# Summing a gate's 128 partial rows with adding transfers instead of a product with ones, and moving two column sums to a later stage

## The reference

```python
mod = jax.nn.silu(c) @ w_ada[l] + b_ada[l]
sh_m, sc_m, gt_m, sh_f, sc_f, gt_f = [m[:, None, :] for m in jnp.split(mod, 6, axis=-1)]

h = rms_norm(x, g_pre_mix[l]) * (1.0 + sc_m) + sh_m
proj = h @ w_in[l]
...                      # attention on one half, convolution on the other
mix = jnp.concatenate([y_attn, y_conv], axis=-1) @ w_out[l]
x = x + gt_m * rms_norm(mix, g_post_mix[l])

h = rms_norm(x, g_pre_ffn[l]) * (1.0 + sc_f) + sh_f
ff = peer_ffn(h, peer_wq[l], ...)   # query projection h @ peer_wq, then expert lookup
x = x + gt_f * rms_norm(ff, g_post_ffn[l])
```

## Time and profile before

| | |
|---|---|
| time, median of 3 runs (range) | 1759.13 us (1758.56 to 1760.4) |
| the profiled execution | 1760.12 us, span 1758.1 us |
| busy: PE, DVE, ACT, POOL | 99%, 87%, 45%, 34% |
| read from HBM over the span | 598.19 MB, 350 GB/s in the mean |

### The profile page before, as it was taken

How to read it: one execution, slowest core, us unless ns; L and a number is a source line. 1 busy time by engine, 2 the same in 40 slices (tenths; PEclk the granted TensorE clock), 3 DMA queues, 4 the chain that set the end, 5 groups by cost and what they waited for, 6 DMA issues and landing times.

```text
span 1758.1 us, 28277 instructions
## 1 busy us (share of the span) xinstructions
PE 1732.3 (99%) x9480; PEld 1517.9 (86%) x9480; DVE 1535.3 (87%) x2469; ACT 799.5 (45%) x1185; POOL 603.1 (34%) x413
## 2 busy tenths in 40 slices
PE   7999999999999999999999999999999999999998
PEld 5888888644999999999999999988888888888886
DVE  4668899967688898998999999989999999999997
ACT  3001222300545555556555555554455544555454
POOL 1000000011000388788688888613321211112110
PEclk9999999999999999999999999999999999999999
DMA  9999986699798777987899999999999999999994
GB/s 380 421 421 422 424 322 252 234 387 417 301 349 272 219 218 223 296 253 224 249 382 389 399 411 404 401 365 411 414 413 410 390 404 398 397 399 389 407 387 190
DMA packets 142648, 617.22 MB, mean 351 GB/s; under 512 B 45347, under 2 KB 45939, under 8 KB 87411
## 3 DMA queue, kind: packets, MB, share of 16 engines
q1 hardware_dynamic: 80530, 410.04, 60.0%
q0 software_dynamic: 55712, 202.52, 31.9%
q10 hardware_dynamic: 6336, 3.75, 0.7%
HBM read 598.19 MB, written 16.89 MB: 350 GB/s over the span
## 4 chain that ended last, share of the span: by engine, by line
PE 76%; DMA 9%; DVE 8%; POOL 4%; issue 2%; ACT 1%; DVEq 0%; ACTq 0%; POOLq 0%; SPq 0%
PE ps L1448 33%; PE ps L1110 14%; PE ps L1117 9%; DMA raw<-in_w_ada 7%; PE ps L1161 5%; PE ps L1331 5%; POOL weights L570 3%; PE ps L1172 2%; DVE raw L1547 2%; PE ps L1103 2%; PE ps L1277 2%; DMA early<-in_w_front 1%; DVE w_low L1489 1%; DVE big L1603 1%; POOL big L555 1%
## 5 line engine op out<-in xcount | busy, mean ns | idle before, releaser
L805 ACT ACTIVATE w_hi<-raw 128x1024 fp32r<-128x1024 f32 x444 | 468.8, 1059 | 458.6 <-PE ps L1448 187.4
L1489 DVE TENSOR_TENSOR w_low<-raw,w_hi 128x1024 fp32r<-128x1024 f32 x444 | 541.5, 1224 | 85.5 <-ACT w_hi L805 77.6
L570 POOL DMA_INDIRECT weights<-sel x192 | 366.0, 1906 | 69.2 <-issue 57.6
L1110 PE MATMUL ps<-a,w_hi 128*128 128x384 f32 x1920 | 383.9, 341 | 0.8 <-issue 0.8
L1110 PEld LDWEIGHTS ps<-a,w_hi 128*128 128x128 f32 x1920 | 326.9, 189 | 1.6 <-issue 1.0
L1448 PE MATMUL ps<-w_low,a 128*128 128x512 f32 x1024 | 273.8, 389 | 0.0
L1448 PE MATMUL ps<-w_hi,a 128*128 128x512 f32 x1056 | 268.1, 389 | 1.5 <-ACT big L918 1.5
L1117 PEld LDWEIGHTS ps<-a,w_low 128*128 128x128 f32 x1920 | 247.1, 191 | 2.6 <-DVE w_low L1489 2.3
L1117 PE MATMUL ps<-a,w_low 128*128 128x192 f32 x1920 | 248.2, 271 | 0.7 <-DVE w_low L1489 0.6
L1448 PEld LDWEIGHTS ps<-w_hi,a 128*128 128x128 f32 x1056 | 198.2, 188 | 42.6 <-ACT big L918 1.6
L1448 PEld LDWEIGHTS ps<-w_low,a 128*128 128x128 f32 x1024 | 192.3, 188 | 39.8
(11 more groups left out here) (240 smaller groups left out, 2008.2 us busy)
## 6 DMA issues: line engine op xcount, KB each, us to landing
raw<-in_peer_u SPq DMA_DIRECT2D x128, 1024.0 KB
raw<-in_peer_v SPq DMA_DIRECT2D x256, 512.0 KB
early<-in_w_front SPq DMA_DIRECT2D x56, 1024.0 KB, 11.4
raw<-in_w_ada POOLq DMA_DIRECT2D x48, 1024.0 KB, 9.6
raw<-in_w_ada SPq DMA_DIRECT2D x32, 1024.0 KB
raw<-in_peer_wq SPq DMA_DIRECT2D x16, 1024.0 KB
big<-in_w_gate_f POOLq DMA_DIRECT2D x16, 1024.0 KB, 6.0
weights<-third SPq DMA_DIRECT2D x16, 768.0 KB, 19.1
```

Of the source, the lines that this page charges most:

```text
L570: gp.indirect_dma_start(weight_elements, bass.IndirectOffsetOnAxis(ap=put_at[:, c:c + 1], axis=0), put_gate[:, c:c + 1], None, compute_op= ...
L805: act.activation(high_at(ph, j), raw[:, s % RING, :], ACT.Copy).then_inc(hi_ready, 1)
L1110: done = pe.matmul(ps[:, b % 2, 0:2 * TD].rearrange("p (m t) -> p m t", m=2), high_at(ph, j)[:, k * P:(k + 1) * P], a_pair[:, kc, :, 0:TD] ...
L1489: dve.tensor_tensor(w_low[:, s % RING, :], raw[:, s % RING, :], high_at(ph, j).bitcast(F32), ALU.subtract).then_inc(lo_ready, 1)
```

## The change

The products with ones go. Seven adding transfers, issued by POOL behind the loads 55 to 58, sum `acc_gate` to one row. ACT then moves this row to DRAM, reads it back as columns [128, 16], DVE multiplies it by the columns of `g_post_mix` (one instruction of [128, 16] instead of four of [128, 512]), ACT writes the product to DRAM and reads it back as a row on all partitions. `g_post_mix` is read as columns, so the copy `g_row` on all partitions goes.

The sums S30 and S31 (the last two blocks of `w_ada`, `DEFERRED = 2`) leave the ring: POOL loads them into `gate_in_ring` when the 78 others are used, and DVE sums them in the query projection, in the places of the first two gate steps; the gate steps move two places back, and two places later in the projection hold two steps each. S29 stands where S31 stood, behind the residual. `mod_columns` makes 15 of 16 columns at its old place and the last one in the projection. `peer_wq` block 1 now waits for S29, the last sum on its ring place.

```diff
+DEFERRED = 2
+N_RING = N_A - DEFERRED
+TWO_GATE_STEPS = (20, 28)
...
-                        sp.wait_ge(mod_used, N_A - SLOTS + block + 1)
+                        sp.wait_ge(mod_used, max(m for m in range(N_RING) if m % SLOTS == block) + 1)
...
-            for n in range(A_GATE, N_A):
+            for n in range(A_GATE, N_RING):
                 gp.wait_ge(mod_used, max(A_GATE, n - SLOTS + 1))
                 gp.dma_start(mod_slots[n % SLOTS], w_ada[n]).then_inc(mod_in[n % SLOTS], 16)
+                if 0 <= n - SLOTS + 1 - MOD_GATES < len(FOLDS_BEHIND):
+                    for fold in FOLDS_BEHIND[n - SLOTS + 1 - MOD_GATES]:
+                        if fold:
+                            gp.wait_ge(gate_sum_ready, 16 * fold)
+                        span = FOLDS[fold]
+                        gp.dma_start(acc_gate[0:span, :], acc_gate[span:2 * span, :], accum_op=ALU.add)\
+                            .then_inc(gate_sum_ready, 16)
...
+            gp.wait_ge(mod_used, N_RING)
+            for d in range(DEFERRED):
+                gp.dma_start(gate_in_ring[:, d % 2, :], w_ada[N_RING + d]).then_inc(gate_f_in[d % 2], 16)
             for g in range(KC):
                 if g < 2:
-                    gp.wait_ge(mod_used, N_A)
+                    gp.wait_ge(late_mod_used, LATE_MODS + DEFERRED + g - 1)
...
-            act.dma_start(g_row, rows[2, :].partition_broadcast(P)).then_inc(g_row_in, 16)
+            act.wait_ge(h_made_first, KC)
+            act.dma_start(mix_g, rows[2, :].rearrange("(p a) -> p a", p=P)).then_inc(g_row_in, 16)
...
             put_y(PAIRS - 1)
-            act.wait_ge(gate_made, 4)
             act.dma_start(gate_g[:, :], rows[3, :].rearrange("(p a) -> p a", p=P)).then_inc(g_row_in, 16)
+            act.wait_ge(gate_sum_ready, 16 * len(FOLDS))
+            act.dma_start(mix_gate_saved, acc_gate[0:1, :]).then_inc(gate_moved, 16)
+            act.wait_ge(gate_moved, 16)
+            act.dma_start(mix_gate, mix_gate_saved[0, :].rearrange("(p a) -> p a", p=P)).then_inc(gate_moved, 16)
+            act.wait_ge(gate_made, 1)
+            act.dma_start(mix_gate_saved[0, :].rearrange("(p a) -> p a", p=P), mix_gate).then_inc(gate_moved, 16)
+            act.wait_ge(gate_moved, 48)
+            act.dma_start(gate_row, mix_gate_saved[0, :].partition_broadcast(P)).then_inc(gate_moved, 16)
...
-            pe.wait_ge(mod_used, MOD_GATES)
             pe.wait_ge(ln_var, 1)
             pe.wait_ge(y_ready, PAIRS)
-            for g in range(4):
-                done = pe.matmul(ps[:, MIX_SECOND[g], :], ones[:, :], acc_gate[:, g * 512:(g + 1) * 512],
-                                 start=True, stop=True)
-            done.then_inc(gate_sum_ready, 1)
             mix_step(0, 7)
-            pe.wait_ge(gate_made, 4)
...
-            column_sums(10, 15)
-            dve.wait_ge(gate_sum_ready, 1)
-            dve.wait_ge(g_row_in, 16)
-            for g in range(4):
-                cols = slice(g * 512, (g + 1) * 512)
-                dve.tensor_tensor(gate_row[:, cols], ps[:, MIX_SECOND[g], :], g_row[:, cols], ALU.mult)\
-                    .then_inc(gate_made, 1)
-            column_sums(15, 22)
-            dve.wait_ge(gate_made, 4)
+            column_sums(10, 18)
+            dve.wait_ge(gate_moved, 32)
+            dve.wait_ge(g_row_in, 32)
+            dve.tensor_tensor(mix_gate, mix_gate, mix_g, ALU.mult).then_inc(gate_made, 1)
+            column_sums(18, 23)
+            dve.wait_ge(gate_moved, 64)
...
-            column_sums(22, 2 * KC - 1)
+            column_sums(23, 2 * KC - DEFERRED - 1)
...
-            column_sums(2 * KC - 1, 2 * KC)
+            column_sums(2 * KC - DEFERRED - 1, 2 * KC - DEFERRED)
             x2_variance(0)
             x2_diagonal(0)
-            mod_columns()
+            mod_columns(slice(0, K_RING), mod_used, N_RING)
...
-                gate_f_step(u - 4)
+                if u < FIRST_PLAIN + DEFERRED:
+                    late_column_sum(u - FIRST_PLAIN)
+                else:
+                    gate_f_step(u - FIRST_PLAIN - DEFERRED)
+                if u == FIRST_PLAIN + DEFERRED:
+                    mod_columns(slice(K_RING, KC), late_mod_used, LATE_MODS + DEFERRED)
```

More of the change, by code:

```diff
@@ L38 @@
 FOLDS = (64, 32, 16, 8, 4, 2, 1)
+FOLDS_BEHIND = ((0, 1), (2, 3), (4, 5), (6,))
 def at(i, step, first):
@@ L94 @@
 MOD_AT = {nth: n for n, nth in enumerate(MOD_ORDER)}
+DEFERRED = 2
+N_RING = N_A - DEFERRED
+K_RING = KC - DEFERRED // 2
+TWO_GATE_STEPS = (20, 28)
+LATE_MODS = CONV_CHUNKS
 MIX_FIRST, MIX_SECOND = (0, 1, 4, 5), (2, 3, 6, 7)
@@ L192, in build_block @@
         gate_row = region(25984, D)
-        g_row = region(28032, D)
         keysT = region(30080, 2, KEYS)
@@ L282, in build_block @@
         gate_cols = macc[:, 0, :]
+        mix_g, mix_gate = modc[:, 0, :], modc[:, 1, :]
         lam_sum, lam_exp, neg_lam = tiny[:, 0:2], tiny[:, 2:4], tiny[:, 4:5]
@@ L324, in build_block @@
             sem("ln_n"), sem("z_ready"))
-        gate_sum_ready, gate_made = sem("gate_sum_ready"), sem("gate_made")
+        gate_sum_ready, gate_made, gate_moved = sem("gate_sum_ready"), sem("gate_made"), sem("gate_moved")
         mix_first = sem("mix_first")
+        late_mod_used = glu_ready
         mix_sq, mix_gated, m_var, m_root = sem("mix_sq"), sem("mix_gated"), sem("m_var"), sem("m_root")
@@ L842, in _ @@
             x2_sqrt(0)
-            act.wait_ge(mod_used, N_A)
+            act.wait_ge(mod_used, N_RING)
             act.wait_ge(mod_f, 1)
@@ L859, in high_chunk @@
                 act.wait_ge(turned, k + 1)
+                if k == K_RING:
+                    act.wait_ge(late_mod_used, LATE_MODS + DEFERRED)
+                    act.wait_ge(mod_f, 2)
                 cols = slice(P if k < FIRST_PLAIN else 0, T)
@@ L1548, in column_sum, with late_column_sum @@
                                          macc[:, group, k:k + 1]).then_inc(mod_used, 1)
+            def late_column_sum(d):
+                nth = MOD_ORDER[N_RING + d]
+                group, k = (nth // A_FFN) * 2 + nth % 2, (nth % A_FFN) // 2
+                dve.wait_ge(gate_f_in[d % 2], 16 * (d // 2 + 1))
+                dve.tensor_tensor_reduce(gate_in_ring[:, d % 2, :], gate_in_ring[:, d % 2, :], c_all, 1.0, 0.0, ALU.mult,
+                                         ALU.add, macc[:, group, k:k + 1]).then_inc(late_mod_used, 1)
             def gate_step(k):
@@ L1744, in gate_tile, with mod_columns @@
                 gate_mix(1, 2 * tt + 1)
-            def mod_columns():
-                dve.wait_ge(mod_used, N_A)
-                dve.tensor_tensor(modc[:, 2, :], macc[:, 2, :], b_col[:, 2, :], ALU.add)
-                link(dve.tensor_tensor(modc[:, 3, :], macc[:, 3, :], b_col[:, 3, :], ALU.add))
-                dve.tensor_tensor(modc[:, 3, :], modc[:, 3, :], g_col[:, 1, :], ALU.mult).then_inc(mod_f, 1)
+            def mod_columns(ks, used, n):
+                dve.wait_ge(used, n)
+                dve.tensor_tensor(modc[:, 2, ks], macc[:, 2, ks], b_col[:, 2, ks], ALU.add)
+                link(dve.tensor_tensor(modc[:, 3, ks], macc[:, 3, ks], b_col[:, 3, ks], ALU.add))
+                dve.tensor_tensor(modc[:, 3, ks], modc[:, 3, ks], g_col[:, 1, ks], ALU.mult).then_inc(mod_f, 1)
             def wq_lo(u):
@@ L1816, in _ @@
                 low_chunk(u)
-                gate_f_step(u - 4)
+                if u < FIRST_PLAIN + DEFERRED:
[4 more added lines that the diff above has]
+                    mod_columns(slice(K_RING, KC), late_mod_used, LATE_MODS + DEFERRED)
+            gate_n = KC - FIRST_PLAIN - DEFERRED
             for u in range(KC, 2 * KC):
                 wq_lo(u)
-                gate_f_step(u - 4)
+                for _ in range(2 if u in TWO_GATE_STEPS else 1):
+                    gate_f_step(gate_n)
+                    gate_n += 1
             def experts(ph, q, i, base, row0):
```

3 lines of the change are left out of this document (2 added, 1 removed).

## The result

The changed kernel takes 1763.61 us (median of 13 runs, lowest 1761.63), the kernel before on the same chips 1758.97 us (13 runs). The ratio is 1.0026, with a 95% interval from 1.0018 to 1.0035: slower by 4.6 us (3.2 to 6.2). One run of the changed kernel was disturbed as a whole (2483 us) and is left out of the ratio. 1755.7 was forecast with a range to 1759.6: the prediction was wrong, in its sign too.

What follows compares the result with a forecast made beforehand. Bound: TensorE's own work behind the seam of mix and query projection, so when TensorE passes it. Gains of 3.3 us there and 0.1 took 1760.12 to 1756.7; the median, 1.0 lower, gave 1755.7, range 1753.6 to 1759.6.

Steps and rivals of the forecast that it cites:

- POOL held by the pairs of adding transfers: POOL's waits with loads queued behind: T 1.0 us later, at most 2.5 (one load more on the way).
- T: Start of `gate_tile(0)` on DVE, before the seam of mix and query projection: 435.23 before, 431.9 forecast.
- the prediction's own signs of being wrong: DMA share clearly below 1 from 352 to 384, S28 ending after 434, TensorE waits for `peer_wq`, L1489 or `w_hi`.
- the idle time at 384 to 392: DMA engines at 0.77 there; 1.84 us of transfer time comes back once DVE's wait for the products goes.
- The products: Four products with ones leave TensorE's path, 3.44 us; mix ends at 438.65 instead of 442.09.
- The gate's way through DRAM: ACT's transfers of the gate end near 406, hidden if before 415.7; the write takes 6.7 us.
- Block 1 of `peer_wq`: Query projection, chunks 2 and 3: lands at T + 11.5 to T + 11.95, stall 0 to 0.2 us.
- Rival (b): Block 1 of `peer_wq` loads at half the rate, 2.5 us later; time 1758.1, chance 0.13.
- (a): Transfers stay the limit at the seam of mix and query projection: T 435.2, TensorE waits 4.7 us; 1759.0, chance 0.17.
- (c): Block 1 of `peer_wq` as late as other loads, median 9.6 us: 1760.5; chance 0.08, half above 0.2% slower.
- (d): TensorE's clock falls while it stands before the query projection, up to 3.7 us lost: 1762.7; chance 0.04.
- The edits costed at nothing: Late sums (up to 2.0 us) and double gate steps (2.6) hidden in DVE's waits; no `g_row`, 0.1 us gained.

Runs made afterwards that it cites:

- sp_loads: Changed kernel with `w_ada` loads 56 to 63 issued by SP between its `w_out` blocks, POOL keeping the adding transfers; ratio 0.9984 to the kernel before.
- deferral alone: Changed kernel with the gate summed by TensorE's four products as before, the two sums still moved to the query projection; ratio 1.0007 to the kernel before.
- the run with fillers: Changed kernel plus 28 products that nothing reads on TensorE ahead of its wait for the diagonal; ratio 1.0022 to the kernel before.
- sp_loads_undeferred: sp_loads with no column sum moved to the query projection (`DEFERRED = 0`); ratio 1.0016 to the kernel before.
- spread: Changed kernel with adding transfers one at a time behind loads 55, 56, 57, 59, 62, 64, 66 instead of in pairs; ratio 1.0035 to the kernel before.
- transfers_only: Changed kernel with the adding transfers but no column sum moved to the query projection (`DEFERRED = 0`); ratio 1.0044 to the kernel before.

## Why the prediction was wrong

**The step that failed** is the term "POOL held by the pairs of adding transfers", +1.0 with a bound of 2.5 us. It measured 7.9 us (T with and without them), and two things were wrong in it. First the length: I ended the hold at about 352.5 from the second gate's chain; it ended at 362.7. The waits were 32.5 us instead of 25.7, each issue about 0.8 instead of 0.53 (that was a load's; the second gate's own adding transfers took 0.77 to 0.89 before), and loads stood between the pairs. The second gate's chain runs with POOL's queue empty of loads, but sp_loads, with a queue as empty, waits 32.7 us too. The DMA engines had somewhat more to do beside it (share 0.75 to 1.02 from 322 to 370 in sp_loads, 0.76 to 0.87 from 556 to 588 before); that this makes the difference isn't shown. Second the bound: "one load more on the way" put a ceiling of one load on a hold that, 10 us long, kept back loads 59, 60 and 61: three loads at 2.49 us, an estimate of 7.5 us. The right question was which loads the kernel before had issued by the time the hold ends, for any end that it could have. Two of the prediction's own signs of being wrong came: the DMA share was 0.79 and 0.89 from 352 to 368, and S28 ended at 437.1.

**The other terms of T held together to 1.7 us.** Without the adding transfers the sum says 431.9 - 1.0 = 430.9; 429.19 was measured. The runs don't part them further, but the idle time at 384 to 392 was indeed filled. The distance from T to TensorE, 8.11, measured 8.10. **The products** went as forecast, mix ending at 438.25 (438.65). That the kernel without adding transfers takes 1755.59, almost the forecast's 1755.7, is luck in part: it passes the seam at 437.94 instead of 440.0, and loses about as much behind it.

**The gate's way through DRAM** took longer than forecast (the write from 397.07 to 406.83, 9.8 us instead of 6.7), and the slack just covered it: `gate_mix` ran at 420.97 without a wait, 16.1 us ahead of T, and the work that stands between fills all but 0.4 us of that. **Block 1 of `peer_wq`**: no wait after; in sp_loads chunks 2 and 3 start at T + 11.85 (441.81 - 429.96) after 0.54 us, inside T + 11.5 to T + 11.95. Rival (b) fails there. In sp_loads POOL issues the two late loads at 437.20, but from 438 to 441 SP's queue alone moves data (0.12, 0.40 and 0.43 MB in each us), and POOL's begins in the us behind that. From 442 to 444 SP's queue moves 0.46 MB and POOL's 0.41. The Trainium skill's rule that each DMA engine takes turns between queues ("DMA: Bandwidth & Descriptors", section on queues, rings and completion order) agrees with that second stretch; what failed is the prediction's estimate from it, which let both loads begin together.

**The rivals.** (a), the transfers as the limit, came nearest in its shape, but its T of 435.2 was my worst case and too early by 1.9 us. (c) didn't happen. (d) did: the clock fell in a long gap at the seam, and it cost 1.05 us, not 3.7. That 3.7 was read off the start of the program, where the granted clock had read 1.00. Whether that was the clock stays open: 16 instructions in 3 us is the pace of the 0.50 windows (11 in 2 us), and the column says otherwise. The Trainium skill ("TensorE: Matmul & The Clock Gate", Part 1) has an idle TensorE fall to 1.2 GHz and come back under work; the windows at 442 to 450 agree, 0.66 and 0.50 to 1.00. The prediction gave that mechanism 0.04, and all cases of a slower kernel 0.08: too little, since all of them hung on a T that I had bounded by one load.

**The edits costed at nothing** cost nothing in the profiled execution after (its last stretch, 455.34 to 1760.5, took 1305.2 us against 1305.7 before). They may not be free in others: in the ratios, deferral alone, sp_loads, the kernel without adding transfers and that with small ones lie 1.5 to 3 us above what the seam of their profiled execution gained, and so does the rest of the 4.6 us here. The profiled executions show it only as single waits at varying places; those in the query projection that stand out (1.11 us in deferral alone, 2.64 us in the run with fillers) come from the second gate's late blocks. The kernel with no deferral on SP has about 2 us of it too, beyond its clock. What causes the rest stays open.

## What to carry to other kernels

A chain of dependent transfers on a queue costs its landing times, and everything that is queued behind it on the issuing engine pays them: before putting such a chain ahead of loads, list which loads went out in that time and multiply by the time of one where the transfers are full. Put the chain on an issuer with nothing behind it, and let it end before the transfers fill up. Work that is moved to a later stage takes its buffers there too: look at what else is loaded into them. A bound is only one if the thing that it counts (here one load) can't come more than once.

## What the runs showed of the hardware

- Seven dependent adding transfers of 64 rows to 1 row of 8 KB cost 32.5 and 32.7 us of waits (runs after and sp_loads); the first (512 KB) landed 10.5 us after its issue. 64 bytes per row in place of 8 KB brought the waits to 17.8. The number of rows hardly tells: the transfer of 256 KB was waited for for 3.83 us, the one of 32 KB for 7.01.
- A product with a single moving column took 0.22 us per instruction in the mean, and TensorE, busy for the whole of it, fell to a granted clock of 0.52.
- A gap of 6.94 us cost 1.05 us behind it, one of 5.43 us 0.6 (453.14 - 443.43 = 9.71 instead of 9.10, run sp_loads_undeferred). But one of 5.19 us cost 1.25 (453.77 - 443.42, run spread) and one of 13.12 us 1.28 (461.82 - 451.44, run transfers_only): in these runs the length of the gap doesn't set the loss.
- POOL's two loads of 1 MB at the seam moved nothing for about 4 us after their issue while SP's queue was moving; then the two queues moved about the same amount (run sp_loads, 437 to 444).
